# First six blocks of every mixer on unscaled pieces, with the normal pieces laid over them, in a two-stack transformer kernel

## The reference, cut to what matters

```python
x = LN1(ALPHA * x + swiglu(x))            # ffn 1
x = LN2(ALPHA * x + token_mixing(x))      # w_in: 34 + 32 column blocks of 128, four branches
x = LN3(ALPHA * x + cross_attention(x, mem))
x = LN4(ALPHA * x + swiglu(x))            # ffn 2
```

## Time and profile before

| what | value |
|---|---|
| median of 3 runs | 2869.8 us (2865.08 to 2870.42) |
| the profiled execution | 2868.27 us, its span 2866.5 us |
| mean granted TensorE clock | 0.975 of full |
| TensorE busy | 2717.7 us (95%), 21805 matmuls |
| GpSimd busy | 2206.3 us (77%) |
| ScalarE busy | 1493.7 us (52%) |
| VectorE busy | 1380.7 us (48%) |

### The profile page before, as it was taken

How to read it: one execution, slowest core, us unless ns; L and a number is a source line. 1 busy time by engine, 2 the same in 40 slices (tenths; PEclk the granted TensorE clock), 3 DMA queues, 4 the chain that set the end, 5 groups by cost and what they waited for, 6 DMA issues and landing times.

```text
span 2866.5 us, 60073 instructions
## 1 busy us (share of the span) xinstructions
PE 2717.7 (95%) x21805; PEld 2623.7 (92%) x21812; DVE 1380.7 (48%) x2501; ACT 1493.7 (52%) x2269; POOL 2206.3 (77%) x1681
## 2 busy tenths in 40 slices
PE   8999999999999999999989989999999899898997
PEld 8999988889999989898889989998999899788997
DVE  2125435646556554525556554346433733735335
ACT  4444455555555545455465554457545644555445
POOL 8876766757988967666858968978898699667994
PEclk9999999999999999999999999999999999999998
DMA  6544434434554544433434544544555355444552
GB/s 242 183 169 151 142 124 135 153 118 155 184 175 158 187 143 170 133 133 133 162 118 155 183 147 162 183 147 159 170 184 187 126 189 185 135 135 148 188 183 78
DMA packets 123000, 452.12 MB, mean 158 GB/s; under 512 B 13650, under 2 KB 13650, under 8 KB 122196
## 3 DMA queue, kind: packets, MB, share of 16 engines
q1 hardware_dynamic: 121104, 441.43, 45.8%
q10 hardware_dynamic: 1732, 8.39, 0.8%
HBM read 448.72 MB, written 1.05 MB: 157 GB/s over the span
## 4 chain that ended last, share of the span: by engine, by line
POOL 45%; PE 25%; issue 23%; DVE 5%; ACT 2%; POOLq 0%; DVEq 0%; ACTq 0%
POOL wl L372 23%; POOL wl L373 22%; PE R L407 6%; PE R L411 6%; PE R L410 6%; PE Y L407 1%; PE Y L411 1%; PE Y L410 1%; DVE M L2260 1%; DVE XLB L1904 0%; ACT wh L1140 0%; PE Y L647 0%; PE R L512 0%; DVE G L2259 0%; PE R L570 0%
## 5 line engine op out<-in xcount | busy, mean ns | idle before, releaser
L372 POOL TENSOR_TENSOR wl<-raw,wh 128x512 fp32r<-128x512 f32 x836 | 1112.3, 1331 | 639.1 <-ACT wh L1140 632.9
L407 PE MATMUL R<-XHB,wh 128*128 128x256 f32 (+1 forms) x4264 | 1218.8, 286 | 15.9 <-DVE XLB L2279 6.2
L411 PE MATMUL R<-XHB,wl 128*128 128x256 f32 (+1 forms) x4264 | 1209.5, 284 | 0.0
L410 PE MATMUL R<-XLB,wh 128*128 128x256 f32 (+1 forms) x4264 | 1205.6, 283 | 0.0
L373 POOL TENSOR_TENSOR wl<-raw,wh 128x512 fp32r<-128x512 f32 x836 | 1144.4, 1369 | 0.0
L1140 ACT ACTIVATE wh<-raw 128x1024 fp32r<-128x1024 f32 x836 | 877.3, 1058 | 298.8 <-PE R L407 218.8
L407 PEld LDWEIGHTS R<-XHB,wh 128*128 128x128 f32 x4264 | 810.9, 190 | 23.7 <-POOL wl L373 10.4
L410 PEld LDWEIGHTS R<-XLB,wh 128*128 128x128 f32 x4264 | 814.1, 191 | 1.8 <-issue 1.0
L411 PEld LDWEIGHTS R<-XHB,wl 128*128 128x128 f32 x4264 | 812.5, 191 | 0.0
L407 PE MATMUL Y<-BH,wh 128*128 128x256 f32 x1408 | 398.0, 283 | 1.3 <-DVE BL L1828 1.3
L411 PE MATMUL Y<-BH,wl 128*128 128x256 f32 x1408 | 396.4, 282 | 0.0
(11 more groups left out here) (402 smaller groups left out, 3187.9 us busy)
## 6 DMA issues: line engine op xcount, KB each, us to landing
raw<-in_stream SPq DMA_DIRECT2D x836, 512.0 KB, 3.3
G<-in_wcmp ACTq DMA_DIRECT2D x2, 2048.0 KB, 7.8
G<-in_mem ACTq DMA_DIRECT2D x2, 1024.0 KB, 7.2
TB<-in_table SPq DMA_DIRECT2D x1, 1312.0 KB, 12.4
X<-in_x SPq DMA_DIRECT2D x2, 512.0 KB, 5.1
out_dram<-X ACTq DMA_DIRECT2D x4, 256.0 KB, 2.2
WS<-in_mix_w ACTq DMA_DIRECT2D x2, 256.0 KB
G<-in_p ACTq DMA_DIRECT2D x2, 256.0 KB, 3.3
```

The source lines that it names most:

```text
L372: pool.tensor_tensor(wl[:, s, 0:512], raw[:, r, 0:512], wh[:, s, 0:512].bitcast(F32), ALU.subtract)
L407: i = pe.matmul(o, wh[w], hi, start=start, stop=False, skip_group_check=True)
L410: pe.matmul(o, wh[w], lo, start=False, stop=False, skip_group_check=True)
L411: i = pe.matmul(o, wl[w], hi, start=False, stop=stop, skip_group_check=True)
```

## The change

In all four mixers the first six blocks are multiplied with unscaled pieces, as in `ffn`: three by `together`, the sum of squares, then three by `dense` (`unscaled_six`). VectorE scales the six outputs by S3. Meanwhile VectorE makes the scaled pieces (for LN in X itself, for RMS in W8, by way of a copy RS of S3 in PSUM) and, while the sixth block still runs, ScalarE writes them over the unscaled ones in XH as soon as TensorE has passed each (`piece_read`), and VectorE the low parts (`low_again`). A second `together` (three blocks; two in `hgrn`) begins the rest on these normal pieces. In `gla` the block order is now lr, k, k, xr instead of xr, lr, k, k. The pieces for the RMS mixers are made while X is added up (`add_y`), and those of the first RMS layer inside the last LN norm. The matmuls that summed the squares of all 8 pieces by themselves go away; two on sums formed by VectorE take their place. In the mixers of the first stack, the six outputs also need the bias part, held in BQ. The asides of the first nine blocks come after the second `together`.

```diff
@@ mixer0_chunks
-    return dict(xr=0, lr=4, k=5, xg=7, q=11, g=13)
+    return dict(lr=0, k=1, xr=3, xg=7, q=11, g=13)
@@ TensorE
+            def unscaled_six(hi, lo, width):
+                together(3, hi, lo, split_ready, width)
+                need(sq_added, 3)
+                for c in range(2):
+                    i = pe.matmul(SQ, ONES, W8[:, c, :], start=c == 0, stop=c == 1, skip_group_check=True)
+                i.then_inc(sum_ready, 1)
+                for _ in range(2):
+                    dense(hi, lo, width=width)
+                dense(hi, lo, width=width, passed=piece_read)
@@ TensorE, mixer
+                unscaled_six(XHB, XLB, T + 2)
                 together(3, XH, XL, split_ready)
-                for c in range(3, Z_N):
+                for c in range(3, 9):
+                    aside(c)
+                for c in range(9, Z_N):
                     dense(XH, XL)
                     aside(c)
@@ TensorE, gla
+                unscaled_six(XH, XL, T)
                 together(3, XH, XL, split_ready)
-                for _ in range(3):
-                    dense(XH, XL)
                 evicted(c["lr"])
...
-                for _ in range(5):
+                for _ in range(2):
                     dense(XH, XL)
                 need(lconv_split)
@@ TensorE, hgrn
-                together(3, XH, XL, split_ready)
-                for _ in range(5):
-                    dense(XH, XL)
+                unscaled_six(XH, XL, T)
+                together(2, XH, XL, split_ready)
                 tokens_major(XH, XL)
@@ ScalarE
+            def piece_again(c, src):
+                act.wait_ge(piece_read, t.up(piece_read))
+                give_dve(act.activation(XH[:, c, :], src, ACT.Copy))
+            def last_again(src):
+                act.wait_ge(chunk_ready, t.value("chunk"))
+                give_dve(act.activation(XH[:, DC - 1, :], src, ACT.Copy))
@@ ScalarE, mixer
-                for c in range(Z_N):
+                late_root(0, keep=True)
+                skip(6)
+                split_next()
+                split_next()
+                biased(0)
+                biased(1)
+                step(biased(2))
+                split_next()
+                for c in range(4):
+                    i = shifted(c)
+                step(i)
+                aside(2)
+                for c in range(4, DC):
+                    i = shifted(c)
+                step(i)
+                split_next()
+                biased(3)
+                biased(4)
+                split_next()
+                for c in range(DC - 1):
+                    piece_again(c, X[:, c, :])
+                biased(5)
+                last_again(X[:, DC - 1, :])
+                split_next()
+                for c in range(6, Z_N):
                     z(c)
-                    aside(c)
+                    if c == 8:
+                        aside(5)
+                        aside(7)
+                    if c > 8:
+                        aside(c)
@@ ScalarE, gla
-                for j in range(4):
-                    split_next()
-                    skip(1)
-                column(c["lr"])
-                column(c["k"])
-                split_next()
+                late_root(1)
+                skip(6)
+                for _ in range(5):
+                    split_next()
+                for j in range(DC - 1):
+                    need(x_scaled)
+                    piece_again(j, W8[:, j, :])
+                need(x_scaled)
+                last_again(W8[:, DC - 1, :])
+                split_next()
+                split_next()
+                skip(1)
                 o = ready_of("gla", "gate")
...
-                plain(Z[:, c["k"] + 1, :])
                 act.preload_act_table_set("natural_log_exp_and_others")
@@ ScalarE, hgrn
+                late_root(1)
                 need(lb_shifted)
                 act.activation(LB[:, 0:2, :], LB[:, 0:2, :], ACT.Exp).then_inc(lb_exp, 1)
+                split_next()
+                split_next()
+                for c in range(3):
+                    from_dve()
+                    forget(c)
+                split_next()
+                split_next()
+                for c in range(3, 5):
+                    from_dve()
+                    forget(c)
+                split_next()
+                for c in range(DC - 1):
+                    need(x_scaled)
+                    piece_again(c, W8[:, c, :])
+                from_dve()
+                forget(5)
+                need(x_scaled)
+                last_again(W8[:, DC - 1, :])
+                split_next()
+                for c in range(6, 8):
                     split_next()
+                    forget(c)
                 act.preload_act_table_set("natural_log_exp_and_others")
@@ ScalarE, main
-                norm(DC, xs, True, 1.0 / D, 0, lambda c: col(f"ln1_b{l}", c), XH, keep=True)
-
+                pieces(lambda c: col(f"ln1_g{l}", c), col(f"ln1_b{l}", 0, DC))
+                skip(1)
                 act.dma_start(WC[:, :, :], wcmp[l]).then_inc(wcmp_landed, 16)
...
-                pieces(lambda c: col(f"ffn_g{l}_0", c))
+                pieces(lambda c: col(f"ffn_g{l}_0", c), table=l > 0)
                 ffn("rms", eps=1)
                 t.up(y_ready, 4)
-                rms()
+                pieces(lambda c: col(f"mix_g{l}", c))
@@ VectorE
+            def scaled_again(gain):
+                step(dve.tensor_copy(RS, S3[:, 0:T]))
+                for c in range(DC):
+                    give(stt(W8[:, c, :], X[:, c, :], col(gain, c), RS, ALU.mult, ALU.mult), x_scaled)
+            def low_again(c, src):
+                from_act()
+                give_pe(tt_(XL[:, c, :], src, XH[:, c, :].bitcast(F32), ALU.subtract))
@@ VectorE, mixer
+                for c in range(3):
+                    scaled(c)
+                step(dve.tensor_copy(RS, S3[:, 0:T]))
+                for c in range(DC):
+                    give(stt(X[:, c, :], X[:, c, :], col(f"ln1_g{l}", c), RS, ALU.mult, ALU.mult), x_scaled)
+                for c in range(3, 5):
+                    scaled(c)
+                for c in range(DC - 1):
+                    low_again(c, X[:, c, :])
+                scaled(5)
+                low_again(DC - 1, X[:, DC - 1, :])
@@ VectorE, gla
-                for j in range(4):
+                def conv(j):
                     m, x = chunk()
                     y = Z[:, 22 + j, :]
+                    if j < 3:
+                        step(tt_(x[:, 0:T], x[:, 0:T], S3[:, 0:T], ALU.mult))
...
+                late_root(RMS_EPS)
+                for z in (c["lr"], c["k"], c["k"] + 1):
+                    m, o = chunk()
+                    take(tt_(Z[:, z, :], o[:, 0:T], S3[:, 0:T], ALU.mult), m)
+                scaled_again("mix_g0")
+                conv(0)
+                conv(1)
+                for j in range(4):
+                    low_again(j, W8[:, j, :])
+                conv(2)
+                for j in range(4, DC):
+                    low_again(j, W8[:, j, :])
+                conv(3)
                 dve.sem_inc(lconv_done, 1)
@@ VectorE, main
-                    norm(DC, xs, True, 1.0 / D, LN_EPS, lambda c: col(f"ln4_g{l}", c), lambda c: col(f"ln4_b{l}", c), None, None)
+                    norm(DC, xs, True, 1.0 / D, LN_EPS, lambda c: col(f"ln4_g{l}", c), lambda c: col(f"ln4_b{l}", c), None, None,
+                         made=lambda c: piece_of_x(c, lambda c: col("ffn_g0_0", c)))
...
-                add_y(1.0, give_act)
-                rms(f"mix_g{l}")
+                add_y(1.0, give_act, lambda c: col(f"mix_g{l}", c))
```

More of the change, by code:

```diff
@@ L2001, in sharpen, with norm @@
                 take(stt(y, u, 1.5, y, ALU.add, ALU.mult), m)
-            def norm(n, src, mean, scale, eps, gain, bias, hi, lo, between=0, behind=0):
+            def norm(n, src, mean, scale, eps, gain, bias, hi, lo, between=0, behind=0, made=None):
                 if mean:
@@ L2441, in hgrn, with scaled @@
                 give(tt_(LB[:, 1, :], l0, LB[:, 2, :], ALU.subtract), lb_shifted)
+                late_root(RMS_EPS)
+                def scaled(c):
+                    m, o = chunk()
+                    give_act(tt_(o[:, 0:T], o[:, 0:T], S3[:, 0:T], ALU.mult))
+                for c in range(3):
+                    scaled(c)
+                scaled_again("mix_g1")
+                scaled(3)
+                scaled(4)
+                for c in range(DC - 1):
+                    low_again(c, W8[:, c, :])
+                scaled(5)
+                low_again(DC - 1, W8[:, DC - 1, :])
                 need(lb_exp)
```

71 lines of the change are left out of this document (46 added, 25 removed).

## The result

| | kernel before | kernel after |
|---|---|---|
| median | 2869.9 us (2865.1 to 2870.4) | 2921.6 us (2919.1 to 2922.9) |
| ratio | | 1.0181, 95% interval 1.0168 to 1.0194 |
| span of the profiled execution | 2866.5 us | 2918.7 us |
| granted TensorE clock | 0.975 | 0.967 |
| TensorE / GpSimd busy | 95% / 77% | 93% / 75% |

A forecast was written before the change was run, and what follows sets the result against it. One serial supply line was taken to bound: ScalarE splits, GpSimd subtracts, TensorE multiplies. 2 x 9.5 (LN) + 12 (GLA) + 11 (HGRN) - 2 (last LN) = +40 on 2868.3 gives 2908.3, forecast 2910, range 2874 to 2925 us.

The forecast's parts named there:

- steps 1 and 4: LN mixer: B3 split only at the root, new wait 5 us; B8 split only after the last piece, new wait 10 us.
- the HGRN paragraph: HGRN mixer: second `together` of two blocks has its low parts at about +33; VectorE's columns start late; +11 us.
- the last one: Prediction's last paragraph, on the profile after: GpSimd ends two waits in each mixer, 5 to 10 us before the seventh block.
- Rival (a): All mixers: splits never bind, B3 and B8 are ready in time, nine blocks run through; 2834 us, chance 0.13.
- (b): Only the hard gaps: steps 2 and 3 hide behind B3 to B5, leaving 5 and 4.2 us; 2878 us, chance 0.13.
- Landmarks of an LN mixer: Times counted from the end of the feed-forward's last matmul, t0; LN mixers lose 9 to 10 us each.
- the first wait: LN mixer, TensorE ahead of B3: 5 us new wait, as ScalarE splits B3 only after the root starts.
- step 2 and 3: LN mixer: ScalarE and VectorE are the chain through rescalings, shifts and laid-over pieces; last piece at +37.5.
- step 3: LN mixer: VectorE's low pieces contend with GpSimd, 425 to 884 ns each, half of seven at the high price.
- GLA: +12 forecast: GLA mixer: late B3 and B8, then the gate behind the ninth block; first token-major matmul +61.5 against +49.3.
- HGRN: +11 forecast: HGRN mixer: VectorE's columns start at +38.5 instead of +18.3, cheaper ones give back some 8 us; `outer(0)` +75 against +64.2.
- Last LN: Last LN before the RMS layers: first product 5 us earlier, VectorE's string ends only 2 us earlier; -2 us.

The follow-up runs named there:

- the three edits: Changed kernel with B3's split ahead of `late_root`, the second `together` as `dense`, and B8's split ahead of the laid-over pieces, in each mixer: 2897.2 us.
- the run with `dense`: Changed kernel with the second `together` of each mixer replaced by as many `dense`, the first taking laid-over pieces as they come: 2893.6 us.
- the last kernel: Kernel before, with the last LN's unscaled pieces made inside the norm and, in LN mixers, B3's split behind the sixth of eight pieces: 2867.7 us.

## Why the prediction was right, point by point

- **Mechanism and sign: right, and shown.** In the LN mixers both waits stand where they were forecast, ended by GpSimd, at 4.67 and 10.37 us against the 5 and 10 of steps 1 and 4. In GLA and HGRN the first one does too (5.96 and 6.06 us against 6). The second is as large as forecast only in GLA (5.18 us), and there VectorE's last low piece ends it and not GpSimd; in HGRN it is 2.03 us, which fits the +33 that the HGRN paragraph has for the second `together` (measured +32.6), and not the 5 to 10 us of the last one. The edits show what the text only argued: the order of ScalarE's splits and the `together` of three. Rival (a) (splits never bind) and (b) (only the hard gaps) fail by the 10.37 us row; its text set 4 us as the sign of (b).
- **Landmarks of an LN mixer.** First product +5.5 (forecast +5.5), B3 +20.3 (+21.5), B5's end +31.7 (+31.3), second `together` +42.0 (+41.2), B8's end +52.6 (+51.3), compression +70.4 (+69.8). The clock of the first three blocks was charged 1.5 us and cost 0.4 (72 matmuls in 9.1 us), with 1.88 us of idle time ahead of them; behind the first wait 1.2 us were charged and 2.7 paid. The two errors nearly cancel, so part of the good match at B5's end is luck.
- **A mis-weighted term.** The sum counted the first wait as part of the loss of B5's end, and it does lie there. But in LN mixers it doesn't set the second start: without it the second `together` starts at +40.6 (244.12 less 203.51) instead of +42.0. What the sum needed was the chain of step 2 and 3, which it also had; the result didn't depend on the first wait's size.
- **Low pieces (step 3).** Seven were put at 4.6 us (half at 425, half at 884 ns); they took 5.00. Their median is 426 ns and the longest 1370: two prices, not a spread. The Trainium skill (SBUF — State Buffer, "Who interferes with whom") has an exclusive lock for the length of an instruction; the trace agrees (1370 ns are one of VectorE's 0.43 and most of one of GpSimd's 1.28). But all seven at the high price, as I read that rule, would be wrong: GpSimd had only one block to subtract there. Taken at 884 ns each they would have been 6.2 us.
- **GLA: +12 forecast, +14.8 measured.** B5's end was exact (+30.5), B8 ended at +46.7 (forecast +46). The failed step is the last one: from the gate to the first token-major product, +61.5 forecast and +63.6 measured. In that stretch stands a new wait of 2.83 us for B10; the one of 2.06 us for ScalarE's `W` behind it is in the kernel before as well. The run with the gate moved shows that its place is worth 6.6 us in the form with the three edits.
- **HGRN: +11 forecast, +15.4 measured.** `outer(0)` was at +76.6 against +75. The columns started 2.8 us later than counted: the low pieces, and three instructions on 8 columns at 1.2 us each that the kernel before did at 0.17 us (two of them) with GpSimd idle. The cheaper columns gave back 10.6 us (22.8 us from the first to the scans before, 12.2 after), where 8 were forecast. Another 3.0 us come behind `outer(0)`, where I counted nothing: part of it is a wait of 0.72 us for the next feed-forward's square sums, and a read of states that takes 3.5 instead of 2.2 us.
- **Last LN:** -2 forecast, -1.7 measured, the first product 5.5 us earlier (forecast 5).
- **What is not settled.** The part of HGRN's last 3 us that is not named above. The 1.7 us in the unchanged feed-forward behind GLA are probably no work of the change: in three kernels whose GLA is that of the kernel before it takes 1.8 to 1.9 us longer too, in two others of them 0.1 or less.

In short: the forecast lay 12 us low. 7 of them are in GLA and HGRN, half of that behind the landmarks at which I stopped counting; 2.3 in the LN mixers; the rest in stretches that no edit touches.

## What to carry to other kernels

When a serial supplier (here ScalarE's split, then GpSimd) works in program order, every instruction put ahead of a split is time taken from the consumer, so list where each split stands before moving anything. A product that starts on several blocks at once also waits for all of them: where pieces trickle in, let each block ask for its own. Removing one of several waits in series says little: single edits here gave 11, 26 and 13 us, all three together 26. And what an edit gains at the start of a stage has to be followed to its end: the dead matmuls' 3.4 us in the first mixer were gone by the next one.

## What was not expected of the hardware

**The clock behind a wait has its own price, and work that nobody reads can buy it back.** 8 dead matmuls in each first wait and 3 to 18 in each second, added to the changed kernel, made it 11 us faster, with the granted clock of the following blocks in the first mixer at 1.00 instead of 0.76 and 0.80. The Trainium skill (TensorE: Matmul & The Clock Gate) describes the clock as gated by activity; the two pairs of windows agree.

**The same code can get a different clock.** The kernels of the three edits, with and without GLA's gate, have identical LN mixers, yet in their profiles the stretch 280 to 400 us had these windows:

```profile
280.00:400.00 120.00, 115.82 (x852) 110.58 (x851) 54.39 (x97) 57.41 (x97) 78.06 (x60) 0.93 0.37 128
```

```profile
280.00:400.00 120.00, 115.82 (x888) 110.32 (x887) 56.31 (x104) 58.45 (x101) 81.73 (x62) 0.97 0.40 138
```

The second (with the gate moved) got 36 more matmuls done in it, and its first LN mixer took 11.9 us less from start to end (843.7 against 855.6). One profile of each kernel can't carry a difference of some us in such a stretch: the trace of the run with `dense` has the first LN mixer 3 us shorter than in the kernel before, and the 11 timed runs with `dense` in the LN mixers alone show no gain.

**Beside GpSimd, VectorE pays for instructions on 8 columns too.** 128x8 operands took 1.2 us instead of 0.17. Scaling a piece with the factor in SBUF went from 0.49 to 1.40 (the last kernel's rows above), while the change's rescaling of X, with the factor in PSUM, stayed at 0.51 us each with GpSimd at work all the time:

```profile
224.02 4.10 DVE L2241 SCALAR_TENSOR_TENSOR X<-X,SM,Y 128x256 f32<-128x256 f32 x8
```

The copy of the factor to PSUM takes 0.43 us. Eight rescalings at 1.40 us would take 11 us instead of 4.1, so it most likely pays; the change without the copy was not run, and this is an estimate from these rows.
